# Reordering the products of a tile, and the PSUM banks behind them, in a hand-ordered hybrid attention layer on one core

## What is computed

```
shift, scale, gate = split(silu(c) @ w_ada + b_ada, 3)
h    = rmsnorm(x, g_pre) * (1 + scale) + shift
gq, gk, gv, gg, ga, sq, sk, sv, sg = split(h @ w_in)      # one input projection, 2832 columns
# gated linear attention: 4 heads, dk 64, dv 128, causal, carries a state S from tile to tile
log_a = log_sigmoid(ga @ w_alpha + b_alpha) / 16
o_gla, S = gla_recurrence(gq * dk**-0.5, gk, gv, log_a, S0)
o_gla = rmsnorm(o_gla, gla_norm_g) * silu(gg)
# sliding-window attention: 8 query / 2 kv heads, hd 64, own chunk of 64 + the one before, learned sinks
o_swa = sink_attention(rope(sq), rope(sk), sv, mask, sinks) * silu(sg)
o    = concat(o_gla, o_swa) @ w_out
y    = x + gate * rmsnorm(o, g_post)
```

## Time and profile before

| | us |
|---|---|
| runs | 1714.31, 1716.46, 1716.52 (median 1716.46) |
| profiled execution: its own time | 1715.52 |
| profiled execution: span | 1713.8 |
| PE busy | 1591.8 (93%) |
| DVE busy | 1079.0 (63%) |
| ACT busy | 593.1 (35%) |
| POOL busy | 365.1 (21%) |
| mean granted clock of TensorE | 0.983 of full |

### The profile page before, as it was taken

One profiled execution on the slowest core, in us unless ns is written; L12 is line 12 of the kernel. 1 busy time (PEld: TensorE's weight loads), 2 busy tenths in 40 slices (PEclk: granted clock), 3 DMA queues, 4 the chain that ended last, 5 costly groups with the idle time before them and its releaser, 6 DMA issues.

```text
span 1713.8 us, 31107 instructions
## 1 busy us (share of the span) xinstructions
PE 1591.8 (93%) x12209; PEld 922.4 (54%) x12209; DVE 1079.0 (63%) x1937; ACT 593.1 (35%) x1812; POOL 365.1 (21%) x505
## 2 busy tenths in 40 slices
PE   8875999999999999999999999999999999999994
PEld 3442555555555555555555555555555555555552
DVE  0684676766666676766666676766666676776653
ACT  0543333333332333333332333333332333333331
POOL 0022222222222122222222121222222121222220
PEclk9988999999999999999999999999999999999997
DMA  8933232222212222222212222222221222222221
GB/s 262 333 87 81 72 72 61 59 70 71 71 47 45 71 71 62 61 68 71 71 50 42 71 71 63 62 65 71 71 54 40 68 71 64 62 64 65 62 53 36
DMA packets 242392, 128.96 MB, mean 75 GB/s; under 512 B 203709, under 2 KB 228758, under 8 KB 242358
## 3 DMA queue, kind: packets, MB, share of 16 engines
q1 hardware_dynamic: 242358, 128.51, 29.3%
HBM read 46.08 MB, written 17.56 MB: 37 GB/s over the span
## 4 chain that ended last, share of the span: by engine, by line
PE 54%; DVE 36%; SPq 3%; issue 3%; DMA 2%; ACT 2%; POOL 0%; DVEq 0%; ACTq 0%; POOLq 0%
PE bank L429 29%; PE pairP L429 20%; DVE etmp L1102 6%; DVE etmp L1094 6%; DVE xs L877 4%; DVE pair_tok L1082 2%; DVE gates L1109 2%; DVE hT L883 2%; DVE gates L955 2%; DVE etmp L1100 2%; PE pairQ L615 2%; SPq L310 2%; PE pairP L631 2%; DMA wo_lo<-in_w_in 1%; DVE aT L1076 1%
## 5 line engine op out<-in xcount | busy, mean ns | idle before, releaser
L429 PE MATMUL bank<-w_hi,hT 128*128 128x512 f16 (+1 forms) x2640 | 749.3, 360 | 8.5 <-DVE gates L955 8.1
L429 PE MATMUL bank<-w_lo,hT 128*128 128x512 f16 (+1 forms) x1320 | 474.7, 360 | 0.0
L429 PEld LDWEIGHTS bank<-w_hi,hT 128*128 128x128 f16 x2640 | 258.0, 98 | 265.9 <-DVE gates L955 11.9
L429 PE MATMUL pairP<-wo_hi,late 128*128 128x512 f16 x1056 | 323.3, 383 | 26.4 <-DVE wo_lo L865 17.2
L429 PE MATMUL bank<-hT,w_hi 128*128 128x128 f16 x2112 | 182.2, 220 | 29.5 <-DVE hT L883 24.4
L429 PE MATMUL pairP<-wo_lo,late 128*128 128x512 f16 x528 | 202.3, 383 | 0.0
L429 PEld LDWEIGHTS bank<-w_lo,hT 128*128 128x128 f16 x1320 | 129.3, 98 | 113.7 <-issue 0.6
L1033 DVE SCALAR_TENSOR_TENSOR stage<-pairP,y_r,stage 128x1024 f32<-128x1024 f32 x33 | 42.4, 1284 | 231.4 <-ACT y_r L665 231.4
L429 PEld LDWEIGHTS pairP<-wo_hi,late 128*128 128x128 f16 x1056 | 104.0, 98 | 153.3 <-issue 21.7
L429 PEld LDWEIGHTS bank<-hT,w_hi 128*128 128x128 f16 x2112 | 161.7, 98 | 45.3 <-DVE hT L883 40.1
L429 PE MATMUL bank<-hT,w_lo 128*128 128x128 f16 x1056 | 179.9, 220 | 0.0
(11 more groups left out here) (197 smaller groups left out, 2191.1 us busy)
## 6 DMA issues: line engine op xcount, KB each, us to landing
x_res<-x_in SPq DMA_DIRECT2D x33, 512.0 KB, 3.5
x_in<-in_x_prompt SPq DMA_DIRECT2D x32, 512.0 KB, 3.5
out<-stage SPq DMA_DIRECT2D x32, 512.0 KB, 2.7
w_hi<-in_w_ada SPq DMA_DIRECT2D x5, 1024.0 KB, 9.4
w_lo<-in_w_ada SPq DMA_DIRECT2D x5, 1024.0 KB, 13.2
wo_lo<-in_w_in SPq DMA_DIRECT2D x5, 1024.0 KB, 11.9
wo_hi<-in_w_in SPq DMA_DIRECT2D x3, 1024.0 KB, 12.4
late<-pair_tok SPq DMA_TRANSPOSE x165, 3.1
```

Of the source, the lines that this page charges most:

```text
L429: last = pe.matmul(out, a(c, i), b(c, j), start=(c == 0 and n == 0), stop=(c == KC - 1 and n == 2))
```

## The change

PE: the order in a tile becomes QK, o, KSG, `turn_x`, SQ, pv, u, V, z, GG, SG, scores, kt/a, out. The output product of t-1 stands at the end of tile t instead of in its middle. o goes to the first half of `pairQ`, pv to the second and u to the first again; bank 6 serves SQ and GG, bank 7 V and SG. o no longer waits for `gg_x` (SQ does, by way of bank 6), SQ no longer for `mix_gla` (u does), pv no longer for `sg_x` (V does), and V no longer for `mix_swa` (scores do). In tile 0 `turn_x` follows the scores, and the spreading of the gate row over the partitions for the sample (`gate_to_rows(2)`) moves from tile 32 to tile 33, ahead of its out.

ACT and DVE: the post-norm of y (`y_stats`, `y_scale`) is done at the start of the next tile but one, for tile t-2; the x statistics, `h_f32`, the high and low half of the next h move to the first half of the tile; the gate chain of GG stands ahead of the scores' maximum, that of SG behind the attention blocks; S is updated after `mix_swa`.

POOL: normalizing x comes first, the residual sum second, the rotation ahead of the value copies.

SP: the store of y (of t-2) and the residual's x come first; that x is now read from DRAM (`x_prompt`) and no longer copied from `x_in`; then the heads' transposes, the x load, and behind it the mixed output's transposes. The transposes of the probabilities wait for `out_mm`, the end of the output product, since they overwrite what it reads.

Number and size of all products, vector operations and transposes of a tile stay as they were.

```
+        o_ps = pairQ[:, 0:512]
+        pv_ps = pairQ[:, 512:1024]
+        u_ps = pairQ[:, 0:256].rearrange("p (b k) -> p b k", b=2)
...
             def turn_probs(c):
+                if c.prev:
+                    sp.wait_ge(sem["out_mm"], c.t)
...
             def program(c):
+                if c.prev2:
+                    sp.wait_ge(sem["y_final"], c.t - 1)
+                    sp.dma_start(y_prompt[0, bass.ds((c.t - 2) * P, P), :], y_buf[c.par]).then_inc(y_stored[c.par], 16)
...
                 if c.prev:
                     pe.wait_ge(sem["probs_dma"], 32 * t)
-                    pe.wait_ge(sem["sg_x"], t)
                     pe.wait_ge(sem["v_keys"], t)
...
                     if c.prev:
-                        pe.wait_ge(sem["mix_gla"], t)
-                    project(bank7, 512, W_SQ, sem["sq_mm"])
...
+                        pe.wait_ge(sem["sg_x"], t)
+                    project(bank7, 512, W_V, sem["v_mm"])
...
+                    pe.wait_ge(sem["sq_ev"], t + 1)
+                    project(bank6, 512, W_GG, sem["gg_mm"])
+                    pe.wait_ge(sem["v_ev"], t + 1)
+                    project(bank7, 512, W_SG, sem["sg_mm"])
...
                 if c.prev:
                     pe.wait_ge(sem["mix_dma"], 48 * t)
-                    if c.after:
-                        pe.wait_ge(sem["gate_row"], 2)
+                    if c.next:
+                        pe.wait_ge(sem["h_f32"], t + 2)
                     else:
-                        pe.wait_ge(sem["h_f32"], t + 1)
+                        pe.wait_ge(sem["y_mul"], t - 1)
```

More of the change, by code:

```diff
@@ L78, in __init__ @@
         self.prev = not (peeled and t == 0)
+        self.prev2 = not (peeled and t <= 1)
         self.cur = not (peeled and t == NT + 1)
@@ new lines, in program @@
+                    for ch in range(2):
+                        for pp in range(2):
+                            for g in range(KVH):
+                                kk = kB if ch else kA
+                                head = 4 * g + 2 * pp
+                                for part in range(2):
+                                    last = pe.matmul(scores[:, 4 * g + 2 * ch + pp, :],
+                                                     qT[:, ch, head:head + 2, :], kk[:, g, part, :],
+                                                     start=(part == 0), stop=(part == 1))
@@ L800, in program @@
-                if not c.cur:
-                    return
-                if c.first:
-                    split_hi([("in", 11)])
-                act.wait_ge(sem["m_neg"], t + 1)
-                if c.prev:
-                    act.wait_ge(sem["p_lo"], t)
-                if c.first:
-                    act.wait_ge(sem["zeroed"], 1)
-                for g in range(GROUPS):
-                    w = CHUNK if c.first and g % 4 < 2 else P
-                    act.activation(probs[:, g, 0:w], scores[:, g, 0:w], ACT.Exp, bias=m_neg[:, g:g + 1],
-                                   scale=HD ** -0.5, accum_out=row_sum[:, g:g + 1])
@@ L823, in program @@
[L823 to L832 removed]
+                    if c.first:
+                        split_hi([("in", 11)])
@@ new lines, in program @@
+                    if c.prev:
+                        act.wait_ge(sem["p_lo"], t)
+                    if c.first:
+                        act.wait_ge(sem["zeroed"], 1)
+                    for g in range(GROUPS):
+                        w = CHUNK if c.first and g % 4 < 2 else P
+                        act.activation(probs[:, g, 0:w], scores[:, g, 0:w], ACT.Exp, bias=m_neg[:, g:g + 1],
+                                       scale=HD ** -0.5, accum_out=row_sum[:, g:g + 1])
+                    act.wait_ge(sem["sink_d"], t + 1)
@@ new lines, in program @@
+                    act.activation(sink_e[:, :], sink_d[:, :], ACT.Exp).then_inc(sem["p_exp"], 1)
+                    act.wait_ge(sem["p_exp"], t + 1)
+                    if c.prev:
+                        act.wait_ge(sem["mix_dma"], 48 * t)
+                    act.activation(pair_tok[:, 0, :], late[:, 0:D], ACT.Copy).then_inc(sem["p_hi"], 1)
+                    if c.first:
+                        h_hi(1, 1)
+                        split_hi([("out", 0), ("out", 1), ("out", 2)])
+                if c.after:
+                    gate_to_stage(2)
+                    act.wait_ge(y_stored[1 - par], 16 * (NT // 2))
+                    y_stats(t, 1 - par)
@@ L967, in program @@
                     v_lo(t, par)
+                if c.next and c.prev:
+                    h_f32(t + 1, int(c.last))
                 if c.second:
@@ L987, in program @@
                                       mix_tok[:, :, 0, :], ALU.subtract).then_inc(sem["mix_lo"], 1)
+                if c.second:
+                    split_lo([("out", 3), ("out", 4), ("out", 5)])
+                if c.next and c.prev:
+                    h_lo(t + 1, 1 - par)
                 if c.cur:
@@ new lines, in program @@
+                    last.then_inc(sem["sg_x"], 1)
+                    dve.wait_ge(sem["p_hi"], t + 1)
+                    dve.tensor_tensor(pair_tok[:, 1, :], late[:, 0:D], pair_tok[:, 0, :], ALU.subtract)\
+                       .then_inc(sem["p_lo"], 1)
+                    if c.first:
+                        h_lo(1, 1)
+                    dve.wait_ge(sem["p_exp"], t + 1)
+                    dve.tensor_tensor(den[:, :], row_sum[:, :], sink_e[:, :], ALU.add).then_inc(sem["den"], 1)
+                    dve.wait_ge(sem["den"], t + 1)
@@ L1111, in program @@
-                last.then_inc(sem["sg_x"], 1)
             all_tiles(dve, program, 2)
```

453 lines of the change are left out of this document (212 added, 241 removed).

## The result

| | before | after |
|---|---|---|
| runs, median (us) | 1716.18 (1714.31 to 1716.52, 4 runs) | 1656.30 (1653.93 to 1657.86, 4 runs) |
| span of the profiled execution | 1713.8 | 1654.2 |
| QK to QK in the loop (30 tiles) | 48.13 | 45.89 |
| tile 0 / tile 1 | 49.03 / 68.17 | 60.12 / 69.65 |
| from the sample's QK to the end | 89.9 | 85.0 |

The ratio is 0.9652, 95% interval 0.9635 to 0.9669. Runs of one kernel lie up to 4 us apart, so smaller differences are read from the stretches in the traces and not from the times. The forecast was 1655, with a range of 1640 to 1680.

The account below looks back on a forecast made before the run. The prediction took PE, busy 93% but waiting three times per tile for DVE's late work, as the bound. Loop -63, tile 0 +11, tile 1 0 and end -8.5 made -60.5, so 1655 us, range 1640 to 1680.

Parts of the forecast that it names:

- Loop: 30 loop tiles: PE's work stays 45.9 us and its waits go, 2.1 us gained per tile, 63 in all.
- three waits: PE's gaps in each loop tile: 0.77 us before QK, 0.73 before pv, 0.25 before SQ, together 1.75 as printed.
- one run: One run of DVE vector work across the boundary of two tiles ends PE's waits; DVE is late there, not full.
- Tile 0: SG must wait for w_in's last part; QK of tile 1 starts at 60 us against 49.0, about 11 dearer.
- Tile 1: SG waits 14.5 us behind w_out's last load and splits; 68 us taken (65 to 71), no change.
- SP comes to the load at about 34.5: Tile 1: SP reaches the load of w_out's last two units about 34.5 us in, behind heads' and mixed output's transposes.
- its own sum of 65: Tile 1: 45.9 of work, 14.5 of SG's wait, 2.3 for its restart and 2.3 for QK's make 65 us.
- two restarts of 2.3: Tile 1: after a long wait PE's clock is lower, 2.3 us per restart, booked once for SG and once for QK.
- The end: From the sample's QK to the end: 81.5 us against 89.9, 8.5 cheaper, the gate row's product hidden under transposes.
- Late transposes: Rival at out: mixed output's transposes land up to 3.8 us late per tile, 114 more, time 1769; chance 0.05.
- Small waits in place of the three: Rival in the loop: part of the gain returns as 1 us of waits per tile, time 1685; chance 0.12.
- The closed loop on DVE: Rival in the loop: the wait moves to another product, period stays 48.13, only the ends change, time 1718; chance 0.04.

Follow-up runs that it names:

- the shortened reciprocal: Kernel before, with the window attention gate's reciprocal taken of 128 of its 512 columns only: 1668.82 us, loop period 46.82.
- the swap: Kernel before, with DVE's low half of the next h put ahead of the low half of the probabilities: 1722.05 us, loop period 48.35.
- the run with all banks: Kernel before, low halves swapped, new banks for o, pv and u, S updated later, out where it stood: 1644.06 us, loop period 45.94.
- the run in 8 pieces: Kernel after, with the load of x issued as 8 DMAs of 16 rows: 1704.86 us, loop period 47.46.
- The run with tile 0's next h forward: Kernel after, in tile 0 turn_x between GG and SG and h of tile 1 right behind GG's gate chain: 1646.65 us.
- The run with the splits moved: Kernel after, with w_out's last splits moved forward and units 6 and 7 loaded ahead of the heads' transposes: 1635.24 us, tile 1 at 48.7.
- three small edits: Kernel after, with gate row ahead of the mixed output's wait, w_out's splits moved and tile 0's next h forward: 1622.04 us, ratio to before 0.9454.

## Why the prediction was right, and where its terms were off

The time came out 1.3 us from the forecast, but this closeness is in part luck, since errors cancel: the loop gave 4.4 us more than forecast, tile 1 and the end 1.5 and 3.6 less.

- **Loop, forecast -63 (52 to 67), measured -67.4.** The mechanism held: three waits go and none takes their place. 2.24 per tile is the whole of the reckoning that adds 0.16 of lost overlap to each printed gap (2.23); the 0.14 that the prediction held back is the error of 4.4, since nothing came in place of the gaps.
- **What each wait hangs on.** That PE waited for DVE's run across the tiles is shown by the shortened reciprocal and the swap. The prediction spoke of one run; there were three stretches in it, those to QK, to o and to pv and SQ, and the one to o, by way of bank 7, it had not seen: it was hidden while QK waited. It also ascribed the gain to the reordering as a whole; the run with all banks shows that the order from V on need not change for it.
- **Margins.** h's low half: 21.5 into the tile forecast, 21.6 measured (809.29 + 1.42 in DVE's row below, with QK at 789.11). p_lo: 47.3 forecast, 45.3 measured. The mixed output's transposes: 2.5 in hand forecast, 2.0 read and 2.2 by the run in 8 pieces.

```profile
809.29 1.42 DVE L897 TENSOR_TENSOR hT<-xs,hT 128x1024 f16<-128x1024 f32 x1
...
833.20 1.23 DVE L1116 TENSOR_TENSOR pair_tok<-late,pair_tok 128x1024 f16<-128x1024 f32 x1
```

- **Tile 0, forecast 60 (+11), measured 60.12.** SG waited 5.1 for the last split and QK 12.9 for h, as worked out. The run with tile 0's next h forward shows that the place of h in tile 0, behind SG's gate chain, was the price: without it the tile took 50.1.
- **Tile 1, forecast 68 with a wait of SG of 14.5, measured 69.65 with 19.4.** The failed step is "SP comes to the load at about 34.5": the row says 165.15, 42.2 into the tile. The step took the last link (the queue's order) and three DVE splits of 1.2, and left out what stands before them: the load of units 3 to 5 waits for DVE's splits of 0 to 2, and the heads' high halves on ACT stand behind the splits of 3 to 5. The run with the splits moved took the whole wait away. That the tile's total came out close is luck: the prediction set its own sum of 65 aside and booked no change. With the measured wait in place of 14.5 that sum, 45.9 and two restarts of 2.3, gives 69.9.
- **The end, forecast -8.5, measured -4.9.** The failed step is "the gate row's product, which moved behind pv, fits under the 5 us of the mixed output's transposes". It cannot: PE takes the wait for those transposes first, and the product is queued behind it. It costs the 4.9 us from 1629.18 to 1634.08, and moving the wait took 4.7 out of the way from pv to out. A cost was taken as covered by a wait that it stands behind.
- **Clock.** The mean granted clock was 0.84 in tiles 0 and 1, with waits of 12.9 and 19.4, 1.00 in the loop, and 0.94 and 0.97 once the first had shrunk to 4.9 and the second was gone. PE is busy for 50.28 us in tile 1 and for 45.89 in a tile of the loop, 4.4 more, where the prediction booked two restarts of 2.3. The Trainium skill (page "TensorE: Matmul & The Clock Gate", section "HAM oscillation — how this bites in real kernels") has groups of matmuls start cold after long waits; the windows agree.
- **Rivals.** Late transposes did not come, but by 2 us only. Small waits in place of the three did not come at all (45.89 in each of 30 tiles). The closed loop on DVE is refuted by the same.

## What to carry to other kernels

When an engine waits at several places in each round, look first whether the waits are ends of one run of work on another engine: then removing one of them moves its time to the next (48.14 and 48.35 for 48.13), and only all of the ends together, or a shorter run, pay. Reckon a gain per round from start to start, not from printed gaps, and list for each product what it waits for next and by how much, since the smallest margin is what the next edit will meet. An order that suits the steady state has to be followed through the first and last rounds by itself: here they took back 7.7 of 67.4 us at first, and three small edits there gave 34 us more.

## What the runs showed of the hardware that was not expected

DVE's busy time fell from 1079.0 to 1005.6 us and POOL's rose from 365.1 to 415.4, with the same operations. Two groups of each kernel show it, from the lists of groups by line (busy us, mean ns), before and then after:

```profile
L1018 DVE COPY fac_in<-bsum 128x2 f32<-128x2 f32 x33 | 58.2, 1764 | 0.0
...
L1151 POOL COPY vA<-vB 64x256 f16<-64x256 f16 x33 | 14.0, 426 | 1.4
```

```profile
L1042 DVE COPY fac_in<-bsum 128x2 f32<-128x2 f32 x33 | 7.0, 213 | 0.0
...
L1193 POOL COPY vA<-vB 64x256 f16<-64x256 f16 x33 | 41.6, 1260 | 1.4
```

These are means of unlike cases. In the kernel before, a DVE copy of two elements took 1.87 us in the 31 tiles in which POOL's normalizing of x ran beside it, and 0.16 in the other two; in the kernel after, it took 0.16 in 32 tiles and 1.87 in the one where they still met. POOL's copies of the values went the other way: 0.40 in 32 tiles before, and 1.30 after in the 30 in which they ran beside DVE's subtractions. One of these (`hT<-xs,hT`, 1.22 before) took 1.42 in just those 30. That DVE and POOL hold each other up where they run side by side is how I read it; no run was made for it. The Trainium skill (page "SBUF — State Buffer", section "Who interferes with whom") says that these two share a pair of ports and that one of them can block the other for a whole instruction, which agrees with these times.
